# The last 256 tokens with tokens on partitions, and a reordered chunk recurrence, in a hybrid decoder layer on one core

## The reference

```python
mix = jnp.concatenate([rg_out, ssd_out, xa_out], axis=-1) @ w_out
res = DEEPNORM_ALPHA * xf + mix
mu = jnp.mean(res, axis=-1, keepdims=True)
var = jnp.mean(jnp.square(res - mu), axis=-1, keepdims=True)
y = (res - mu) * lax.rsqrt(var + LN_EPS) * ln_g + ln_b
```

```python
seg = acum[:, :, :, None] - acum[:, :, None, :]
decay = jnp.exp(jnp.where(causal, seg, -inf))
y_diag = einsum(cb, decay, xs)          # within the chunk
y_off = einsum(cc, h_in, exp(acum))     # from the state before it
s_y = y_diag + y_off + ssd_d * s_x      # the last term is the skip
```

## Time and profile before

| | us |
|---|---|
| median of 3 runs | 1198.63 (1198.3 to 1199.48) |
| profiled execution, its own time | 1196.54 |
| its span | 1194.6 |
| TensorE busy | 1172.1 (98%) |
| VectorE busy | 584.2 (49%) |
| ScalarE busy | 441.8 (37%) |
| GpSimd busy | 349.6 (29%) |
| mean granted clock of TensorE | 0.996 of full |

### The profile page before, as it was taken

One profiled execution on the slowest core, in us unless ns is written; L12 is line 12 of the kernel. 1 busy time (PEld: TensorE's weight loads), 2 busy tenths in 40 slices (PEclk: granted clock), 3 DMA queues, 4 the chain that ended last, 5 costly groups with the idle time before them and its releaser, 6 DMA issues.

```text
span 1194.6 us, 17909 instructions
## 1 busy us (share of the span) xinstructions
PE 1172.1 (98%) x7577; PEld 1105.2 (93%) x7577; DVE 584.2 (49%) x756; ACT 441.8 (37%) x725; POOL 349.6 (29%) x221
## 2 busy tenths in 40 slices
PE   9999999999999999999999999999999999999996
PEld 9999999899999999877899989999998889999995
DVE  7666666643157776676622475111003543444256
ACT  5666645632133323544344452111123322322124
POOL 2112111113212121677574561221220002224332
PEclk9999999999999999999999999999999999999999
DMA  7111110136221101112332334624101232345012
GB/s 289 45 45 40 58 40 19 41 127 210 85 76 38 51 18 42 71 71 78 136 113 94 119 106 155 185 91 171 53 1 71 107 142 90 123 152 180 26 56 91
DMA packets 43727, 110.71 MB, mean 93 GB/s; under 512 B 5584, under 2 KB 26208, under 8 KB 41216
## 3 DMA queue, kind: packets, MB, share of 16 engines
q1 hardware_dynamic: 26560, 87.93, 20.7%
q10 hardware_dynamic: 17088, 21.64, 5.9%
HBM read 89.32 MB, written 20.24 MB: 92 GB/s over the span
## 4 chain that ended last, share of the span: by engine, by line
PE 86%; ACT 4%; DVE 4%; issue 2%; POOL 2%; DMA 1%; ACTq 0%; SPq 0%; POOLq 0%; DVEq 0%
PE bank L674 25%; PE bank L676 24%; PE bank L675 24%; PE bank L848 2%; PE bank L1076 2%; PE bank L1087 2%; POOL mix L625 2%; ACT k_sk L1365 1%; ACT k_L L1374 1%; DVE k_EA L1803 1%; DVE k_EA L1805 1%; PE bank L1064 1%; PE bank L1099 1%; ACT o_res L1536 1%; PE bank L1120 1%
## 5 line engine op out<-in xcount | busy, mean ns | idle before, releaser
L578 POOL TENSOR_TENSOR wlo<-wraw,whi 128x1024 fp32r<-128x1024 f32 x84 | 214.0, 2552 | 702.8 <-ACT whi L1168 702.8
L674 PE MATMUL bank<-xh,whi 128*128 128x352 f32 x1224 | 398.3, 325 | 2.7 <-issue 1.1
L676 PE MATMUL bank<-xh,wlo 128*128 128x352 f32 x1224 | 392.6, 321 | 0.0
L675 PE MATMUL bank<-xl,whi 128*128 128x352 f32 x1224 | 392.5, 321 | 0.0
L674 PEld LDWEIGHTS bank<-xh,whi 128*128 128x128 f32 x1224 | 229.6, 188 | 8.9 <-issue 5.9
L675 PEld LDWEIGHTS bank<-xl,whi 128*128 128x128 f32 x1224 | 230.1, 188 | 0.9
L676 PEld LDWEIGHTS bank<-xh,wlo 128*128 128x128 f32 x1224 | 229.7, 188 | 0.0
L674 PE MATMUL bank<-o_mh,whi 128*128 128x352 f32 (+2 forms) x456 | 148.5, 326 | 1.4 <-ACT z_ss L1398 0.6
L676 PE MATMUL bank<-o_mh,wlo 128*128 128x352 f32 (+2 forms) x456 | 147.6, 324 | 0.0
L675 PE MATMUL bank<-ml,whi 128*128 128x352 f32 (+2 forms) x456 | 147.0, 322 | 0.0
L1168 ACT ACTIVATE whi<-wraw 128x1024 fp32r<-128x1024 f32 x87 | 92.1, 1060 | 122.6 <-DVE o_part L1612 82.9
(11 more groups left out here) (288 smaller groups left out, 1737.6 us busy)
## 6 DMA issues: line engine op xcount, KB each, us to landing
wraw<-in_w_stream SPq DMA_DIRECT2D x92, 512.0 KB, 3.3
partial<-o_part ACTq DMA_DIRECT2D x48, 176.0 KB, 1.9
b_kv<-in_cache_k SPq DMA_DIRECT2D x8, 1024.0 KB, 4.8
b_kv<-in_cache_v SPq DMA_DIRECT2D x8, 1024.0 KB, 4.8
mix<-in_xT SPq DMA_DIRECT2D x8, 528.0 KB, 7.7
o_part<-in_xT ACTq DMA_DIRECT2D x24, 176.0 KB, 2.8
o_part<-partial ACTq DMA_DIRECT2D x24, 176.0 KB, 2.6
wraw<-in_h0T SPq DMA_DIRECT2D x8, 512.0 KB, 3.2
```

Of the source, the lines that this page charges most:

```text
L578: nc.gpsimd.tensor_tensor(lo_of(n), wraw[:, n % RAW, :], hi_of(n).bitcast(F32), ALU.subtract).then_inc(lo_done, 1)
L674: mm(out, lh, rh, start=first, stop=False)
L675: mm(out, lh, rl, start=False, stop=False)
L676: return mm(out, ll, rh, start=False, stop=last)
```

## The change

1. **The last 256 tokens.** `LN_COLS` keeps two ranges, up to column 800. The rest is made by tokens: two halves r of 128 tokens each. The stationary operand is now the activation (`o_mh2`, `ml`), 128 tokens wide, and the weights stream, in groups of three, two and three 128-channel pieces (`TAIL_GROUPS`), so that a token's channels lie along a row of PSUM. At k = 0 of each group fp32 products of `o_res` with the identity add the residual. VectorE takes `bn_stats` of each piece and `bn_aggr` over all, ScalarE the root, VectorE the reciprocal and two operations per group that scale a row and write it to `wraw`; SP stores it to a new output `y_tail`. Gain and offset are needed as rows: `t_gb`, a broadcast load of 1 MB that ScalarE starts after the first range's root. The last piece of the second range is stored by ScalarE's queue.
2. **The recurrence.** ScalarE makes the skip copies after the exponentials; `k_EA`'s exponential waits for `k_out` in their place. From the second chunk step on ScalarE copies the mask into banks 2 and 3 (new semaphore `k_fut`) and TensorE's segment product adds to it, so the two mask products per step are gone. GpSimd makes `e_bm` of step e+1 ahead of the skip add of step e-1.
3. **The start.** The 20 products of `ones` are gone.

```diff
@@ TensorE, out_normalised
+                for r in range(TAILS):
+                    tok = slice(TAIL + r * P, TAIL + r * P + P)
+                    for g, (a, b) in enumerate(TAIL_GROUPS):
...
+                        pe.wait_ge(out_added, 6 * NT + n - 5)
+                        if r == 0 and g == 0:
+                            pe.wait_ge(mix_lo, 3 * NT + 1)
+                            pe.wait_ge(res_in[-1], 16)
+                        for k in range(NT):
...
+                            mm(out, o_mh2[:, k, tok], wh, start=k == 0, stop=False, skip_group_check=True)
+                            mm(out, o_mh2[:, k, tok], wl, start=False, stop=False, skip_group_check=True)
+                            last = mm(out, ml[:, k, tok], wh, start=False, stop=k == NT - 1, skip_group_check=True)
+                            if k == 0:
+                                for ob in range(a, b):
+                                    mm(bank[:, (n + 3) % 6, (ob - a) * P:(ob - a + 1) * P], o_res[:, ob, tok], ident[:],
+                                       start=False, stop=False, skip_group_check=True)
+                            if k == 4 and r == 1 and g == 0:
+                                squares(len(LN_COLS) - 1)
+                        last.then_inc(t_ready, 1)
+                        if r == 0 and g == 0:
+                            sums(len(LN_COLS) - 1)
-            pe.wait_ge(const_set, 1)
-            for i in range(WARM):
-                mm(bank[:, 7, 0:P], ones[:], ones[:], start=True, stop=True)
@@ TensorE, before_scan
+                if e > 2:
+                    pe.wait_ge(k_fut, e - 2)
...
+                    if e > 2:
+                        last = mm(o, s_acs[:, tk], k_n[:, g, b, :], start=False, stop=True, skip_group_check=True)
+                        continue
@@ ScalarE, phase K
-                    if e >= 4:
-                        act.wait_ge(k_out, e - 3)
-                    for t in range(4):
...
-                    last.then_inc(k_skip, 1)
                     act.wait_ge(k_turned, e + 1)
...
                 act.wait_ge(k_bcast, e + 1)
+                if e >= 4:
+                    act.wait_ge(k_out, e - 3)
                 fn(k_EA[:, g] if e >= 2 else e_EA[:, e], bank[:, 7, 0:4 * q].rearrange("p (t i) -> p t i", t=4),
                    ACT.Exp).then_inc(k_ea, 1)
+                if 2 <= e < STEPS - 1:
+                    act.wait_ge(k_exp, e + 1)
+                    fn(bank[:, 2:4, :].rearrange("p a (h i) -> p (a h) i", i=Q),
+                       s_maskr[:].bitcast(F32).unsqueeze(1).to_broadcast([P, HG, Q]), ACT.Copy).then_inc(k_fut, 1)
+                if e >= 2:
+                    for t in range(4):
...
+                    last.then_inc(k_skip, 1)
@@ ScalarE, end
+                if i == len(LN_COLS) - 1:
+                    tail_deviation(0)
...
                 for n, obs in ln_pieces(i):
+                    if n == sum(LN_PIECES) - 1:
+                        tail_deviation(1)
                     act.wait_ge(ln_norm, n + 1)
@@ GpSimd, phase K
                 if e > 2:
                     decay_prompt_state(e - 1)
+                    if e < STEPS - 1:
+                        batch_b(e + 1)
                     add_skip(e - 1)
@@ VectorE, end
+            tail_stats(0, 0)
+            centre(last, 0)
+            centre(last, 1)
+            tail_stats(0, 1)
+            add_squares(last)
+            tail_stats(0, 2)
+            tail_moments(0)
+            tail_rows(0)
+            tail_stats(1, 0)
+            inverse(last)
+            normalise(last, 0)
+            normalise(last, 1)
+            tail_stats(1, 1)
+            tail_stats(1, 2)
+            tail_moments(1)
+            tail_rows(1)
```

More of the change, by code:

```diff
@@ L313, in hybrid_step @@
         part_out = [sem(f"part_out{i}") for i in range(PARTS)]
-        res_in, y_out = [sem(f"res_in{i}") for i in range(len(LN_COLS))], sem("y_out")
+        res_in, y_out = [sem(f"res_in{i}") for i in range(len(LN_COLS) + 1)], sem("y_out")
+        t_ready, t_var, t_std, t_y = sem("t_ready"), sem("t_var"), sem("t_std"), sem("t_y")
         const_set, d_zero = sem("const_set"), sem("d_zero")
@@ L661, in _ @@
             for i, (c0, w) in enumerate(LN_COLS):
-                for ob in range(1, NT - (i == LN_LAST)):
+                for ob in range(1, NT):
                     pool.wait_ge(out_added, 6 * NT + NT * i + ob + 1)
@@ L811, in out_normalised @@
                             squares(i - 1)
-                c0, w = LN_COLS[LN_LAST]
-                pe.wait_ge(ln_acc, (NT - 1) * LN_LAST + NT - 2)
-                mm(bank[:, 6, 0:w], ones[:], o_acc[:, LN_LAST, 0:w], start=True, stop=False)
-                pe.wait_ge(out_added, 6 * NT + NT * len(LN_COLS))
-                mm(bank[:, 6, 0:w], ones[:], o_res[:, NT - 1, c0:c0 + w], start=False, stop=True).then_inc(ln_mean, 1)
-                for n, obs in ln_pieces(LN_LAST):
-                    pe.wait_ge(ln_sqd, n + 1)
-                    for ob in range(obs.start, obs.stop):
-                        last = mm(bank[:, 7, 0:w], ones[:], o_sq[:, ob, 0:w], start=ob == 0, stop=ob == NT - 1)
@@ L1537, in _ @@
                     last.then_inc(ln_y, 1)
+            act.wait_ge(ln_y, sum(LN_PIECES))
+            c0, w = LN_COLS[-1]
+            obs = ln_pieces(len(LN_COLS) - 1)[-1][1]
+            act.dma_start(O["y"][:, obs, c0:c0 + w], o_res[:, obs, c0:c0 + w]).then_inc(y_out, 16)
         @block.vector
```

103 lines of the change are left out of this document (76 added, 27 removed).

## The result

The changed kernel takes 1183.38 us (median of 4 runs, 1182.02 to 1184.16), the kernel before 1198.47 (4 runs, 1197.0 to 1199.48). The ratio is 0.9874, with a 95% interval from 0.9858 to 0.989: 15.1 us less. The forecast was 1184.1, 14.5 less. The profiled execution took 1182.02, as the sum of the prediction had it, and that is in part luck: the term for the end was off by 1.3, and 1.0 us that no term of the sum had made up for most of it.

The account below looks back on a forecast made before the run. The prediction took TensorE's product stream as the bound, except in the chunk recurrence's loop and at the end. Its terms -10.4 - 4.8 + 0.7 = -14.5 gave 1182.0 profiled, 1184.1 us as median, range 1180.8 to 1190.5.

Parts of the forecast that it names:

- Part 1, the recurrence: Chunk recurrence, phase K: a step falls from 6.39 to 5.70 us, 15 steps give -10.4 (bounds -11.4 to -7.4).
- The loop that was cut: Recurrence step before: a closed loop through VectorE, GpSimd's skip add and ScalarE's skip copies and exponential, 6.40 us.
- TensorE's floor: Recurrence: TensorE's own work per step, 6.06 us before and 5.63 without the two mask products.
- state loop: Recurrence: GpSimd scales the sample state after the skip add, VectorE adds to it before its decay multiply; 5.69 to 5.77 us.
- The cover of the mask copy: Recurrence: ScalarE's mask copy hides up to about 3.5 us before TensorE needs it; beyond that each microsecond lies on every step.
- e_bm "costs nothing": Recurrence, GpSimd: e_bm (0.36 us) moved ahead of the skip add fits into the 1.15 us GpSimd waited there.
- Part 2, the end: Last 256 tokens: the new end finishes at 1189.8 in place of 1194.6, -4.8 us (bounds -6.5 to -1.8).
- the last store issued by ScalarE: Sign for the end: ScalarE's 800 KB store, 3.7 us, lands last, at 1189.8.
- the two stores share their queue time: Rival at the end, with VectorE late as its alternative: the -4.8 is gone, 1188.9 us; chance 0.10.
- Part 3, the start: Start of the kernel: without the 20 products of ones TensorE's first products run at half rate, +0.7 us (+0.3 to +2.0).
- The recurrence's wait moved: Rival in phase K: mask copy, TensorE's wait or GpSimd's queue binds at about 6.05 us, 1189.3; chance 0.13.
- The clock rival: Recurrence: TensorE's clock falls to 1.2 GHz, steps of 9.7 us, slower than before, up to 1248; chance 0.04.

Follow-up runs that it names:

- a_copy4: The changed kernel with ScalarE's mask copy made four times, each waiting for the one before: 1199.83 us.
- a_nostore: The changed kernel without ScalarE's 800 KB store at the end (computed but not written): 1181.03 us.
- a_warm: The changed kernel with the 20 products of ones back at the start: 1183.75 us.
- a_end: The changed kernel with its last 800 KB store in halves, two of ScalarE's last four scalings ahead of its last small root: 1182.0 us.
- b_mask: The kernel before with only the mask copied by ScalarE in place of the two mask products, skip copies still first: 1196.27 us.
- b_order: The kernel before with only the order on ScalarE changed (skip copies behind the exponentials), mask products and e_bm as they were: 1192.57 us.
- a_copy2: The changed kernel with ScalarE's mask copy made twice, the second waiting for the first: 1183.03 us.
- b_recur: The kernel before with the whole recurrence change (order on ScalarE, mask copy, early e_bm) and nothing else: 1186.75 us.

## Why the prediction was right, and where not

- **Part 1, the recurrence** (predicted -10.4, measured -10.5 in the traces, -10.8 in the medians with that part alone). The loop that was cut, the loop that came next and TensorE's floor right under it were all as worked out: state loop 5.67 (predicted 5.69 to 5.77), mask copy 1.03 (1.01), 0.83 us left in front of the skip add (about 0.8). TensorE's own pace is 5.59 where 5.63 stood, so the two limits lie 0.08 apart, and the slower one binds.
- **The cover of the mask copy** was put at 3.5 us, from when TensorE needs it. The runs put it at 3.0, by ScalarE's queue in a_copy4. The step that failed is that only the consumer was looked at: ScalarE's own queue is full sooner. The sum of that queue (3.9 us, in the prediction) already had it.
- **e_bm "costs nothing"** in its new place holds. That it had to be moved the prediction has in its loop of 5.7, but it gives no price: left in place it costs 5.1, half of the part.
- **Part 2, the end** (predicted -4.8; measured -3.5 between the two traces, -4.1 with the shorter end, -3.9 as the only change). Product stream: +3.6. The prediction has 4.0 for the 16 products with the identity and 3.8 for the shift of the last product, and does not say what the 0.2 between them are; by their starts these products take 3.1, 0.19 each where I took 0.25. Deviation ready 1.5 after the last product: 1171.0 to 1172.47. VectorE's rows 3.4, ScalarE's scalings 2.54 (2.5). VectorE was in time, with 0.9 us of idle in front of its last statistics (0.3 predicted). The term that was mis-sized is the last one, the stores. I took the 800 KB as the last to land, 3.7 us after ScalarE's issue; it took 4.1, and the small store issued 1.0 after it took 3.8 and landed last, so the sign "the last store issued by ScalarE" did not come. The prediction had this among its rivals ("the two stores share their queue time") and priced it at the whole of part 2. It costs 1.9, or 1.4 by the shorter end (a_nostore). By its own mark, 9 us behind the last product, the part was wrong in size in this trace, 9.2, and 0.4 inside the mark in the four with the shorter end.
- **Part 3, the start** (predicted +0.7, bounds +0.3 to +2.0). The profiled execution shows +0.67, with the step in the rate at about 10.6. But that execution was a lucky one. The second unit's start in all seven traces without the products of ones: 20.40, 20.36, 20.50, 20.63, 21.36, 21.49, 21.49; in the seven with them: 19.46 to 19.86. The mean cost is 1.3, near the middle of the bounds, and the last three lie 1.6 to 1.8 behind the 19.73 of before, over the mark of 1.5 for being wrong. Against it stand the 0.8 by which the kernels without these products are shorter behind phase K. The prediction has no such term, and it says that nothing behind the start is slack; a_warm, whose median is 0.4 above the changed kernel's and not 0.67 below it, is in line with that, with runs that scatter over 2 us. In the profiled execution the gain behind phase K and the 0.35 ahead of it hide most of the 1.3 by which the end fell short: the sum fits to 0.1 by luck. In a_end the slow starts go on to 12.71:

```profile
11.83 1.09 PE L726 MATMUL bank<-xh,wlo 128*128 128x352 f32 x3
12.71 0.53 PE L719 MATMUL bank<-xh,whi 128*128 128x352 f32 x2
```

  The Trainium skill, "TensorE: Matmul & The Clock Gate", section "What's actually happening", says that the number of slow products at the start differs from run to run; these traces agree, with 10 to 21 products at half rate.
- **The rivals.** The recurrence's wait moved, but to the loop of 5.67 that the forecast had, and not to the rival's 6.05. It would have been 6.03 to 6.06 with either the mask copy or e_bm left out. The clock rival, slower than before, did not occur: from 500 us to the last product the clock is full. Two rows of the changed kernel, for the earlier trace rows:

```profile
475.00:500.00 25.00, 23.57 (x208) 20.17 (x207) 16.95 (x35) 16.63 (x36) 14.77 (x20) 0.93 0.12 44
500.00:575.00 75.00, 73.57 (x627) 59.18 (x626) 58.17 (x92) 48.46 (x102) 62.78 (x78) 1.00 0.27 99
```

  Its place was right all the same: the 0.93 at the beginning of phase K is the changed kernel's one loss of granted clock between its start and its last product, and it varies by 1.5 us; and in a_copy4, with steps of 6.85, the clock did fall inside the loop.

What stays open: why the low stretch is sometimes twice as long or comes twice, and whether the products of ones make that more likely; why the kernels with these products take 0.8 longer behind phase K; why the end takes 36.0 or 36.6. All four runs of a_warm have a mean clock of 0.995, all four of a_end 0.997, with only that difference and the order of the end between them; but the kernel before, b_mask and b_order, which have those products, show 3.4 us at the lower clock, and a_copy2 and a_copy4, which have not, show 6.8. It was not tried to give TensorE more to do ahead of that stretch; by an estimate from its length at half rate (3.4 or 6.8 us), 1.7 to 3.4 us are the most that could be had. Nor was a cheaper way to add the residual, whose 16 products take 3.1 of the end.

## What to carry to other kernels

When a wait is cut out of a loop over several engines, write down the next two limits as well, each as a closed sum: here they lay at 6.06 and 6.03 under a loop of 6.39, and two edits, of which neither shortened the step on top of the new order alone, were worth 5.8 us together. How much an added operation may cost is the smaller of two numbers, the time until its reader needs it and the idle time of its own engine's queue. At the very end of a kernel, count bytes and not stores: a large store that is started just ahead of the last small one delays it, and half of it sent earlier from an idle stretch gave most of that back here.

## What was not expected of the hardware

- A 192 KB store lands in 1.9 us without the 800 KB (a_nostore), and in 3.8 or 3.2 when an 800 KB store from another queue was issued 1.0 us ahead of it; together they move 383 to 390 GB/s.
- Behind phase K, with nearly the same code there, the kernels that had 20 products of ones at their start take 0.8 us longer: 575.58 to 576.51 us in seven traces against 574.86 to 575.37 in seven without. Of the 1.3 that dropping them costs at the start, 0.5 are left.
- TensorE fell to 1.2 GHz at the beginning of phase K in every kernel here, for about 3.4 us or for about 6.8. Phase K with the same code gives both (the changed kernel and a_warm), which alone is 1.5 us between two executions. In the 16 runs of the kernel before beside b_recur the time follows the mean clock, which also counts what happens behind the last product: 1194.97 at 0.997, 1196.3 to 1197.0 at 0.996, 1198.1 to 1199.8 at 0.993 to 0.995. With a scatter of that size an edit of 0.7 us can't be told by the time of a few runs, and a trace can tell it only where it acts.
